# A decoder layer on one core: attention keys projected with the weights stationary and rotated in pieces of 512 columns

## The reference, cut to what matters

```
u = rms_norm(h, norm_gain)
q_a, k_a, v_a, g_a, q_i, k_i, w_i, q_r, k_r, v_r, g_r = split(u @ w_in)
q_a, k_a = rotary(q_a), rotary(k_a)       # 8 heads x 64, only dims 0..15 turn
    # dims 0..7:  x1 * cos - x2 * sin ;  dims 8..15:  x2 * cos + x1 * sin
sel = top_k(indexer_score(q_i, k_i, w_i), 128)   # per query, causal
y_a = softmax(q_a . k_a[sel] / 8) @ v_a[sel] * silu(g_a)
y_r = retention(rotary(q_r), rotary(k_r), v_r) * silu(g_r)
h   = h + concat(y_a, y_r) @ w_out ;  out = rms_norm(h, final_gain)
```

## Time and profile before

| | us |
|---|---|
| median of three runs | 280.79 |
| the profiled execution, its own time | 280.87 |
| its span, first to last instruction | 279.1 |
| PE busy | 271.7 (97%) |
| PE weight load busy | 227.0 (81%) |
| DVE busy | 200.5 (72%) |
| ACT busy | 157.2 (56%) |
| POOL busy | 64.2 (23%) |
| mean granted clock of PE | 0.999 of full speed |

### The profile page before, as it was taken

How to read it: one execution, slowest core, us unless ns; L and a number is a source line. 1 busy time by engine, 2 the same in 40 slices (tenths; PEclk the granted TensorE clock), 3 DMA queues, 4 the chain that set the end, 5 groups by cost and what they waited for, 6 DMA issues and landing times.

```text
span 279.1 us, 4372 instructions
## 1 busy us (share of the span) xinstructions
PE 271.7 (97%) x1493; PEld 227.0 (81%) x1493; DVE 200.5 (72%) x419; ACT 157.2 (56%) x331; POOL 64.2 (23%) x116
## 2 busy tenths in 40 slices
PE   8999999999999999999999999999999999999992
PEld 8988888888878788787888888788788888888891
DVE  3786889999999997999696663685656825563342
ACT  4896755536455423767658646776675694241231
POOL 2036622322300059767300102103020020000211
PEclk9999999999999999999999999999999999999999
DMA  7999504220422045052204220040120275111223
GB/s 267 403 400 350 154 4 150 75 76 2 150 76 78 0 150 150 2 150 73 80 2 150 75 78 0 6 147 23 59 73 0 77 237 177 36 41 38 78 88 139
DMA packets 13989, 30.10 MB, mean 108 GB/s; under 512 B 1168, under 2 KB 1680, under 8 KB 13968
## 3 DMA queue, kind: packets, MB, share of 16 engines
q1 hardware_dynamic: 13392, 29.04, 31.2%
q10 hardware_dynamic: 576, 0.79, 0.7%
HBM read 27.73 MB, written 2.10 MB: 107 GB/s over the span
## 4 chain that ended last, share of the span: by engine, by line
PE 67%; DVE 24%; DMA 3%; issue 2%; ACT 2%; SPq 1%; POOLq 0%; DVEq 0%; ACTq 0%
PE bank L527 14%; PE bank L529 13%; PE bank L528 13%; DVE keys L1263 6%; DVE top L1261 6%; DVE w_lo L1150 5%; PE bank L594 4%; PE bank L610 3%; PE bank L523 3%; DMA x_h<-in_first 3%; PE bank L524 3%; PE bank L525 3%; DVE k_stack L1224 2%; PE bank L626 2%; PE bank L625 2%
## 5 line engine op out<-in xcount | busy, mean ns | idle before, releaser
L527 PE MATMUL bank<-w_hi,xT_hi 128*128 128x512 f32 (+1 forms) x264 | 104.2, 395 | 0.1
L529 PE MATMUL bank<-w_hi,xT_lo 128*128 128x512 f32 (+1 forms) x264 | 101.5, 384 | 0.0
L528 PE MATMUL bank<-w_lo,xT_hi 128*128 128x512 f32 (+1 forms) x264 | 101.2, 383 | 0.0
L529 PEld LDWEIGHTS bank<-w_hi,xT_lo 128*128 128x128 f32 x264 | 49.6, 188 | 10.2
L527 PEld LDWEIGHTS bank<-w_hi,xT_hi 128*128 128x128 f32 x264 | 49.7, 188 | 9.8 <-issue 0.7
L528 PEld LDWEIGHTS bank<-w_lo,xT_hi 128*128 128x128 f32 x264 | 49.7, 188 | 8.8
L1150 DVE TENSOR_TENSOR w_lo<-w_raw,w_hi 128x1024 fp32r<-128x1024 f32 x35 | 43.9, 1276 | 13.1 <-ACT w_hi L736 12.8
L736 ACT ACTIVATE w_hi<-w_raw 128x1024 fp32r<-128x1024 f32 x35 | 36.6, 1055 | 6.9 <-PE bank L529 5.0
L1261 DVE MAX8 top<-keys 128x8 f32<-128x256 f32 (+2 forms) x48 | 26.8, 558 | 1.3
L1087 POOL TENSOR_TENSOR th<-zt,tab 128x64 f32<-128x64 f32 (+1 forms) x24 | 12.8, 535 | 62.2 <-ACT zt L791 57.7
L1263 DVE MATCH_REPLACE8 keys<-top,keys 128x256 f32<-128x256 f32 (+2 forms) x48 | 26.0, 542 | 0.0
(11 more groups left out here) (173 smaller groups left out, 442.2 us busy)
## 6 DMA issues: line engine op xcount, KB each, us to landing
w_raw<-in_w_in SPq DMA_DIRECT2D x27, 512.0 KB, 3.8
w_raw<-in_w_out SPq DMA_DIRECT2D x8, 512.0 KB, 3.6
retT<-in_x SPq DMA_DIRECT2D x8, 256.0 KB, 3.4
x_h<-in_first SPq DMA_DIRECT2D x2, 836.0 KB, 8.2
out<-x_h SPq DMA_DIRECT2D x4, 320.0 KB, 2.5
mix<-in_first SPq DMA_DIRECT2D x3, 418.0 KB, 5.3
v_ret<-in_x SPq DMA_DIRECT2D x2, 512.0 KB, 10.4
v_att<-in_x SPq DMA_DIRECT2D x2, 512.0 KB, 12.1
```

The costliest lines, as they stand in the source:

```text
L527: pe.matmul(o, xh, hi[:, kk, c0:c0 + w], start=first, stop=False)
L528: pe.matmul(o, xh, lo[:, kk, c0:c0 + w], start=False, stop=False)
L529: mm = pe.matmul(o, xl, hi[:, kk, c0:c0 + w], start=False, stop=last)
```

## The change

Three things change.

1. **Keys with weights stationary.** For chunk 2, as for the attention gate, the weight block is loaded and the 512 tokens stream. A slot's result now holds 128 key columns (two heads) for all tokens, already turned. ACT copies it without scale into `keys_raw` (the memory of `v_ret`, idle until slot 20). No transposes of keys are left. The row of half rstd values, built on PE and ACT in slot 15 before, is built in slot 10, and POOL's part of it ahead of slot 4.
2. **Rotation in pieces of 512 columns.** The rotating dims now lie on partitions. A table (new input `key_table`, loaded by SP into `prob_odd`) has cos and sin for them, 2 and 0 elsewhere. After slot 11, ACT issues four DMAs within SBUF that copy each half's partner rows from `keys_raw` to `keys_swapped` (memory of `x_h`, set to zero by POOL beforehand). POOL multiplies the two tables by half rstd, then the partner rows by sin (four instructions), DVE the rows by cos in slot 13 (four, `key_cosine`), POOL adds (four). In slot 16 ACT rounds into `k_stack` (`key_hi`, four) and DVE writes the low part (`key_lo`, four, 64 x 1024 each, both operands in SBUF).
3. **Rounds spread.** 3 rounds in each of slots 6 to 12, then 2 in slots 13 to 25 and 1 in slot 26.

```diff
-        n = min(4 if g <= 9 else 3 if g <= 15 else 2, ROUNDS * (MT - 1) - done)
+        n = min(3 if g <= 12 else 2, ROUNDS * (MT - 1) - done)
...
+        keys_raw = v_ret
+        keys_swapped = x_h[0:TURNED, 0:2, :].rearrange("p m (a t) -> p (m a) t", a=2)
+        key_cos, key_sin = prob_odd[:, 0, :], prob_odd[:, 1, :]
...
+                if u == APART + RAW:
+                    sp.wait_ge(wlo_done, APART + 1)
+                    sp.dma_start(prob_odd[:, :, :].rearrange("p a t -> p (a t)"), key_table).then_inc(key_table_in, 16)
...
-                    if c == C_AG:
+                    if c in (C_K, C_AG):
...
-                if g == ATT0 - 1:
+                if g == MT * C_K + 2:
                     turn_rstd()
...
+            def swap_keys():
+                act.wait_ge(z_done, SWAP_AT)
+                act.wait_ge(swapped_zeroed, 1)
+                for hh in range(2):
+                    for x in range(2):
...
+                        act.dma_start(keys_swapped[to, :, :], keys_raw[of, :, :]).then_inc(swapped_in, 16)
+
+            def key_hi(hh):
+                act.wait_ge(key_roped, PAIRS)
+                for half in range(2):
+                    act.activation(k_stack[0:64, hh + 4 * half:hh + 4 * half + 3:2, :],
+                                   keys_raw[64 * hh:64 * hh + 64, 2 * half:2 * half + 2, :], ACT.Copy).then_inc(khi_done, 1)
...
+            def rope_keys():
+                pool.wait_ge(key_table_in, 16)
+                pool.wait_ge(rstd_row_done, 1)
+                for t in (key_cos, key_sin):
+                    pool.tensor_tensor(t, t, half_rstd_row[:, :], ALU.mult).then_inc(key_table_done, 1)
+                pool.wait_ge(key_table_done, 2)
+                pool.wait_ge(swapped_in, 16 * 4)
+                for n in range(PAIRS):
+                    pool.tensor_tensor(keys_swapped[:, n, :], keys_swapped[:, n, :], key_sin[0:TURNED, :],
+                                       ALU.mult).then_inc(key_sined, 1)
+                z = keys_raw[0:TURNED, :, :]
+                for n in range(PAIRS):
+                    pool.wait_ge(key_cosed, n + 1)
+                    pool.wait_ge(key_sined, n + 1)
+                    pool.tensor_tensor(z[:, n, :], z[:, n, :], keys_swapped[:, n, :], ALU.add).then_inc(key_roped, 1)
...
-            def key_lo(m):
...
+            def key_cosine():
+                dve.wait_ge(key_table_done, 1)
+                dve.wait_ge(swapped_in, 16 * 4)
+                for n in range(PAIRS):
+                    dve.tensor_tensor(keys_raw[:, n, :], keys_raw[:, n, :], key_cos, ALU.mult).then_inc(key_cosed, 1)
+
+            def key_lo(hh):
+                for half in range(2):
+                    heads = slice(hh + 4 * half, hh + 4 * half + 3, 2)
+                    dve.wait_ge(khi_done, 2 * hh + half + 1)
+                    dve.tensor_tensor(k_stack[64:128, heads, :], keys_raw[64 * hh:64 * hh + 64, 2 * half:2 * half + 2, :],
+                                      k_stack[0:64, heads, :].bitcast(F32), ALU.subtract).then_inc(klo_done, 1)
```

More of the change, by code:

```diff
@@ L120, in tables, with key_tables @@
     return t
+def key_tables():
+    t = np.zeros((2, 2, HD, SEQ), np.float32)
+    inv = np.float32(1.0) / (np.float32(ROPE_THETA) ** (np.arange(ROPE_HALF, dtype=np.float32) / np.float32(ROPE_HALF)))
+    ang = (inv[:, None] * np.arange(SEQ, dtype=np.float32)[None, :]).astype(np.float32).astype(np.float64)
+    t[0] = 2.0
+    for x, sign in ((0, -2.0), (1, 2.0)):
+        t[0, :, x * ROPE_HALF:(x + 1) * ROPE_HALF] = 2.0 * np.cos(ang)
+        t[1, :, x * ROPE_HALF:(x + 1) * ROPE_HALF] = sign * np.sin(ang)
+    return np.ascontiguousarray(t.reshape(2, P, SEQ).transpose(1, 0, 2).reshape(P, 2 * SEQ))
 def first_chunk(x, norm_gain, w_in):
@@ L186, in transposed, with hymba_layer @@
     c = g // MT
-    if g < 0 or g >= GROUPS or c not in (0, 1, 2, C_RQK):
+    if g < 0 or g >= GROUPS or c not in (0, 1, C_RQK):
         return None
-    return g if c < 3 else g - MT
-def hymba_layer(nc, x, w_in, w_out, final_gain, table, first, out):
+    return g if c < 2 else g - 2 * MT
+def hymba_layer(nc, x, w_in, w_out, final_gain, table, first, key_table, out):
     with ExitStack() as ctx:
@@ L541, in transpose_group @@
                     pe.wait_ge(t_evac, i)
-                if i == 3 * MT:
+                if i == 2 * MT:
                     pe.wait_ge(rstd_row_done, 1)
-                if 2 * MT < i <= 3 * MT:
-                    pe.wait_ge(klo_done, i - 2 * MT)
                 for j in range(4):
@@ L575, in turn_rstd @@
                 pe.wait_ge(rstd_spread, 1)
-                pe.wait_ge(t_evac, 3 * MT)
-                pe.wait_ge(klo_done, MT)
+                pe.wait_ge(t_evac, 2 * MT)
                 for m in range(MT):
@@ L788, in project_out @@
                         act.wait_ge(t_done, i - 1)
-                    if i >= 3 * MT + 2:
-                        act.wait_ge(kz_done, i - 3 * MT - 1)
+                    if i >= 2 * MT + 2:
+                        act.wait_ge(kz_done, i - 2 * MT - 1)
                     act.activation(zt[:, g % 2, :], src[:, :], ACT.Copy, scale=scale).then_inc(z_done, 1)
+                elif c == C_K:
+                    if m == 0:
+                        act.wait_ge(sq_act, 3)
+                        act.wait_ge(sq_dve, 1)
+                    act.activation(keys_raw[:, m, :], src[:, :], ACT.Copy).then_inc(z_done, 1)
                 elif c in (C_V, C_RV):
+                    if c == C_RV and m == 0:
+                        act.wait_ge(klo_done, 4)
                     dst = (v_att if c == C_V else v_ret)[:, m, :]
@@ L823, in transposed_out @@
                     return
-                if c == 2:
-                    for hh in range(2):
-                        ins = act.activation(k_stack[0:64, hh::2, t], mid_ps[64 * hh:64 * hh + 64, :].rearrange(
-                            "p (a t) -> p a t", a=PAIRS), ACT.Copy)
-                    ins.then_inc(t_evac, 1)
-                    return
-                if i == 3 * MT:
+                if i == 2 * MT:
                     act.wait_ge(idx_mm, IDX_HEADS * (MT - 1))
@@ L952, in _ @@
                     relus(g - MT - 1)
-                if g == ATT0 - 1:
+                if g == MT * C_K + 2:
                     rstd_row()
+                if g == SWAP_AT:
+                    swap_keys()
+                if g == SWAP_AT + 4:
+                    key_hi(0)
+                    key_hi(1)
                 if g < GROUPS:
@@ L1083, in _ @@
                 for s in range(2):
-                    if i == 4 * MT - 1 and s:
+                    if i == 3 * MT - 1 and s:
                         pool.wait_ge(q_lo_done, 2)
@@ L1217, in index_lo @@
                                   ALU.subtract).then_inc(idx_lo_done, 1)
-            def key_lo(m):
-                t = slice(m * P, (m + 1) * P)
-                dve.wait_ge(t_evac, 2 * MT + m + 1)
-                for hh in range(2):
-                    ins = dve.tensor_tensor(k_stack[64:128, hh::2, t], mid_ps[64 * hh:64 * hh + 64, :].rearrange(
-                        "p (a t) -> p a t", a=PAIRS), k_stack[0:64, hh::2, t].bitcast(F32), ALU.subtract)
-                ins.then_inc(klo_done, 1)
+            def key_cosine():
[9 more added lines that the diff above has]
+                                      k_stack[0:64, heads, :].bitcast(F32), ALU.subtract).then_inc(klo_done, 1)
             def block_q_lo(b):
```

42 lines of the change are left out of this document (29 added, 13 removed).

## The result

| | before | after |
|---|---|---|
| median, us | 280.77 (280.07 to 281.21) | 289.03 (288.73 to 289.30) |
| the profiled execution | 280.87 | 288.73 |
| its span | 279.1 | 286.9 |

The ratio is 1.0298, with a 95% interval of 1.028 to 1.0317. Both medians are of four runs. The change makes the kernel 8.3 us slower; the forecast was 288.6 us with mechanism A (POOL and DVE take turns in slots 13 to 17, and rounds in slot 25 delay retention).

What follows compares the result with a forecast made beforehand. PE's own work (busy 97%) was taken to set the end, with DVE's chain without room up to the first maximum. 280.87 + 4.5 early + 3.2 late = 288.6 us; range 280.0 to 291.5.

Steps and rivals of the forecast that it cites:

- mechanism A: The forecast itself: turns at slots 13 to 17 and the chain at slot 25, 288.6 us; chance 0.46.
- Early +4.5: First probabilities reach PE at 116.7 against 112.22, 4.5 us late through DVE's chain, PE's saving included.
- late +3.2: Rounds moved behind slot 22: slot 25's two delay retention's chain by 3.0 us, slots 23 and 24 add 0.2.
- the second stretch of turns: POOL's first retention rotation, from 101.4, takes turns with DVE's four low parts of the keys, which end at 109.0.
- PE's saving: Four groups of four transposes fewer in the key slots, 0.49 us per four: 2.0 us.
- Turns on POOL and DVE: From 76.1, POOL and DVE instructions with two SBUF inputs block each other whole; POOL's eight end at 89.4.
- without turns -7.3: Bound on the sum: if POOL and DVE did not take turns, 7.3 us less.
- Slot 16: PE stalls 3.4 us there for unit 18's low part from DVE, ready at 97.6, wanted at 94.1.
- Slot 17: PE asks for the keys' low parts at 105.7, ready at 109.0: 3.4 us more stall.
- The swap: After slot 11, ACT issues four DMAs of about 0.4 us each, landing 2.8 us later, all in at 76.1.
- Rival E: Partner rows land late, holding up DVE's cosines and the work behind them: 298.2 us; chance 0.05.
- Nothing, or up to 1 us if slot 4's rotation is made late: Cost of POOL's copy and memset of the partner rows, placed where POOL waits for ACT.

Runs made afterwards that it cites:

- e3: The changed kernel with POOL's memset of the partner rows moved behind its rotations of the query tiles: 287.77 us.
- e6: The changed kernel with POOL's eight key instructions on 32 of the 512 columns, the rest left out of the computation: 282.36 us.
- e4: The changed kernel with the four sines and four additions of the keys' rotation on DVE instead of POOL: 287.82 us.
- e5: The changed kernel with DVE's work reordered so POOL's sines run beside rounds, queries' low parts behind units 18 and 19, additions after all cosines: 284.47 us.
- e2: The kernel before with only the change's rounds table (3 in slots 6 to 12, then 2): 282.05 us.
- e10: The changed kernel with only slot 25's two rounds moved on DVE, ahead of retention's output instead of behind it: 286.20 us.

## Why the prediction was right

**The sum.** Early +4.5 and late +3.2 were forecast; at slot 20 the kernel after is 4.97 us behind, and slots 27 and 28 add 2.94. That the total came within 0.4 us is in part luck: 1.1 us of the early term is slot 6's stall, which was not forecast and was carried on to the probabilities. Without it (e3) the kernel is 3.85 us behind at slot 20 and takes 287.77 us, 0.8 below the forecast. What made up for it is the second stretch of turns. POOL's rotation for retention was to begin at 101.4 and began at 105.50, so it met only the later low parts of the keys: turns were forecast to add 1.8 us to those four, and they added 0.9 (1.22, 1.21, 1.65 and 1.65 us).

**PE's saving.** 2.0 forecast, 2.1 measured in slots 11 to 15, in every kernel with the new keys.

**Turns on POOL and DVE.** Forecast 13.3 us for POOL's eight (76.1 to 89.4), measured 13.75 (78.04 to 91.8). By "without turns -7.3" the forecast priced both stretches together; e6 measured 6.7 less without the first. e4, e5 and e6 each take turns of the first stretch away in another way, and none agrees with an explanation by DVE's number of instructions alone. What was not in the forecast is that rounds do not take turns (e5).

**The stalls.** Slot 16: 3.4 forecast, 3.6 measured. Slot 17: 3.4 forecast, 0.25 measured. This step failed, and without harm to the sum: PE reached slot 17 at 104.09 instead of 100.3, 2.4 us of it by the slower clock behind the stall in slot 16 and 1.2 by coming late to slot 16 already. So it asked for the keys' low parts 3.8 us later than forecast, just when they were done (109.6; forecast 109.0). The masked maximum, which the chain on DVE sets, came at 113.25 (forecast 112.7). e4 shows the missing stall where slot 16 has none. The other executions of the kernel after have a mean clock of 0.992 and 0.993 against 0.986 in the profiled one, and are no faster (288.86 to 289.30 against 288.73).

**The swap.** Landed 1.9 us later than forecast. Slot 11 ended 1.2 us later, by slot 6's stall, but the issues did not wait for unit 16's rounding to end, so they began only 0.2 later than forecast (71.93 against 71.7). The rest is in the issues. The timeline of ACT's queue in the kernel after:

```profile
71.93 3.20 ACTq L865 DMA_DIRECT2D x_h<-v_ret  x4
```

Four issues take 3.20 us, 1.6 forecast; the last landed 2.9 us behind them, 2.8 forecast. Rival E would have needed a landing later than DVE's arrival; POOL waited, DVE did not.

**The memset.** "Nothing, or up to 1 us if slot 4's rotation is made late" was mis-sized and had the wrong path: 1.3 us (e3), by blocking a DVE instruction and not by making POOL late. I had applied the rule of turns to POOL's arithmetic and not to its memset.

**The late rounds.** The mechanism, the place and the size hold: 2.96 us in e2 and 2.9 in e10 by slots 27 and 28. PE's wait for retention's scores in slot 28 is 1.4 us (forecast about 1.3), and the gate comes 2.9 us later behind retention's output (forecast 3). The forecast had seen that slot 25's place is no hole, but not that the hole stood one instruction ahead of it.

## What to carry to other kernels

Before work is given to POOL to free DVE, ask what DVE does in the same microseconds: the two ran side by side with rounds and with operands in PSUM, and in turns with two operands in SBUF, so the order of DVE's queue is worth as much as the split of the work, and here more (4.6 us less in e5, 1.2 in e4). In a queue with waits, filler belongs directly ahead of the instruction that waits, never directly behind it: the same two rounds cost 3.0 us there and nothing here. And a memset on an idle engine is work too: look at what runs beside it.
